# Low parts one chunk sooner in a layer and an output projection, and the short convolution's first root behind the last decays

## The chip, the cores and the metric

The kernel runs on one core of one Trainium2 chip. The metric is the device time of one execution in microseconds. Three runs before the change took 1665.22, 1665.50 and 1666.05 us (median 1665.5).

## The reference

The input is a sequence of 256 tokens (width 1024) with 256 context tokens. A first block has two layers of attention, each followed by a feed-forward part with a three-tap convolution in its gate. A second block has one layer (a chunked state-space scan beside a short-convolution branch), then a mixture of 16 experts. The parts that the change touches:

```python
def conv_ffn(h, w_gate, w_up, conv_w, conv_b, w_down):
    g = h @ w_gate
    gp = jnp.pad(g, ((0, 0), (1, 1), (0, 0)))
    g = gp[:, :-2] * conv_w[0] + gp[:, 1:-1] * conv_w[1] + gp[:, 2:] * conv_w[2] + conv_b
    return (jax.nn.silu(g) * (h @ w_up)) @ w_down

def short_conv_branch(gate_b, gate_c, h, conv_w, norm_g):
    v = causal_dwconv(gate_c * h, conv_w)
    return group_rmsnorm(gate_b * v, norm_g, SC_GROUPS)      # 16 groups of 64 columns

    proj = u @ w_in[l]
    y_ssd = ssd_branch(...)
    y_sc = short_conv_branch(proj[..., o_dt:o_b], proj[..., o_b:o_c], proj[..., o_c:], sc_conv_w[l], sc_norm[l])
    h = h + jnp.concatenate([y_ssd, y_sc], axis=-1) @ w_out[l]
```

`group_rmsnorm` divides each group of columns by the root of its mean square; all is in fp32.

## The kernel before

Everything lies with features on the 128 partitions and tokens along the free axis: 512 or 256 tokens in the first block, 272 (16 extra tokens in front) in the second. A weight matrix comes in chunks of 1 MB (128 x 2048) or 704 KB (128 x 1408) into a ring of three slots. A product in fp32 is made of three cheaper ones: the weight is split into a high part `WH` (a rounded copy, made by ScalarE in `act_high`, L514) and a low part `WL` (weight minus high part, made by VectorE, DVE for short, in `dve_low`, L524), and the activations into `HH` and `HL`. TensorE adds high x high (L539), high x low (L540) and low x high (L541).

There is no scheduler. Each engine's program is written out by hand in the order in which it runs, with semaphore waits on named marks. `act_high(e, n)` makes the high parts up to chunk n + 2; it waits until the chunk has landed and until TensorE has used the chunk three before it. `dve_low(e, n)` makes the low parts up to chunk n + 1; a third argument moves this end. A wait for a high part inside `dve_low` holds up all that DVE has behind it.

**The feed-forward part of the second layer** (256 tokens, `pe_ffn`, `act_ffn`, `dve_ffn` with l = 1, 915 to 1120 us in the trace). There are 22 gate/up chunks f in two halves of 11; each gives one tile of 128 hidden features, 48 matmuls. A stage f is, on ScalarE: the high part of chunk f + 2, the convolution's middle tap (L980), silu (L985), the high part of the product (L989), and in stages 0 to 7 a residual put off until there (L784). On DVE: a low part, the two outer taps (L1009, L1012), the product with the up half (L1016, once TensorE is through with chunk f), the low part of the product (L1019). After 11 chunks come eight down chunks; the first of them needs all 11 hidden tiles, one after the other, and waits for each tile's L1019.

**The end of the scan** (1225 to 1345 us). `pe_second_half` computes 24 tiles of the input projection, three for each of eight short-convolution tiles x, and runs `pe_scan(f - 1)` after tile f; `act_scan` and `dve_scan` are the same steps on the other engines. From step 5 on, a step starts the decays of one of 16 heads and finishes the output of an earlier one; the last decays, of head 15, are in step 20. When the squares of the tiles x = 0 to 5 are summed (L2151, one 16 x 272 row block), ScalarE takes the root (L2170) and DVE the reciprocal (L2176), both at the head of step 20. TensorE spreads the result (L2192) in steps 21 and 22, ahead of what else these steps hold; DVE and ScalarE normalise with it and split it (L2210, L2200, L2205). The root needs another activation table than the decays' exponential. Tiles 6 and 7 have a form by quarters: the 272 tokens are cut in four pieces of 68, each on 32 partitions of its own (L2160, L2187).

**The output projection** (`pe_wout`, `dve_wout`, `dve_last_tiles`). Its second half (k from the short convolution) comes first, in four chunks. Two of them are begun without tiles 6 and 7, whose sums, root (L2167), reciprocal (L2176) and spread (L2187) come in between; the state-space branch's group norm (L2458, L2464, L2520, L2555) is spread behind them.

Of the kernel before, what the change touches and what calls it, by code (L numbers as in the profile page):

```python
# [10 lines left out]
ACT = mybir.ActivationFunctionType  # L11
# [6 lines left out]
NT = 272  # L18
# [303 lines left out]
class Marks:  # L322
# [10 lines left out]
    def up(self, name, *key):  # L333
        signal = name.split(".")[0]
        assert self.home.setdefault(signal, self.engine) == self.engine, name
        n = self.count[signal] = self.count.get(signal, 0) + 1
        assert self.value.setdefault((name,) + key, n) == n, (name, key)
        return (self.final[signal] if self.final else None), 1

    def at(self, name, *key):  # L340
        if not self.final:
            return None, 1
        return self.final[name.split(".")[0]], self.value[(name,) + key]
# [38 lines left out]
def build(nc, wts, xin, meta, vecs, conds, csts, out):  # L382
# [3 lines left out]
    index = {key: n for n, (key, _) in enumerate(plan)}  # L386

    with ExitStack() as ctx:
# [48 lines left out]
        def C(name, n=None):  # L437
            return cst[:, cat[name][0]:cat[name][0] + (n or cat[name][1])]

        def B(*key):  # L440
            return ps[:, banks.of[key], :]
# [74 lines left out]
        def dve_low(e, n, ahead=2):  # L516
            short = plan[n][0][0] == "gu" and n + 1 < len(plan) and plan[n + 1][0][0] == "mod"
            for i in range(low_at[0], min(n + (3 if short else ahead), len(plan))):
                low_at[0] = i + 1
                if whole[i]:  # L520
                    continue
                hi, lo = split_parts(i)
                e.wait_ge(*at("high", i))
                e.tensor_tensor(lo, raw(i), hi.bitcast(F32), ALU.subtract).then_inc(*up("low", i))  # L524
# [440 lines left out]
        def through(l, f):  # L965
            return index["gu", l, f + 2] + 1 - index["gu", l, f]
# [29 lines left out]
        def dve_ffn(e, F_, gt_from, fold_next=None):  # L996
            l, n = F_.l, F_.n
            H2 = ffn_parts(n)
            nh = n // 256
            for half in range(2):  # L1000
                for i in range(HALF):
                    f = HALF * half + i
                    z = f % 3
                    c = index["gu", l, f]
                    g3 = B("gate", l, f)[:, 0:n].rearrange("p (s t) -> p s t", s=nh)
                    t3 = F_.T[:, z, :].rearrange("p (s t) -> p s t", s=nh)
                    dve_low(e, c, through(l, f) if f < 2 else 2)
                    e.wait_ge(*at("middle", l, f))
                    e.scalar_tensor_tensor(out=t3[:, :, 1:256], in0=g3[:, :, 0:255], scalar=V(f"cw{l}", f),  # L1009
                                           in1=t3[:, :, 1:256], op0=ALU.mult, op1=ALU.add).then_inc(*up("conv", l, f, 0))  # L1010
                    e.wait_ge(*at("conv", l, f, 0))
                    e.scalar_tensor_tensor(out=t3[:, :, 0:255], in0=g3[:, :, 1:256], scalar=V(f"cw{l}", 44 + f),  # L1012
                                           in1=t3[:, :, 0:255], op0=ALU.mult, op1=ALU.add).then_inc(*up("conv", l, f, 1))
                    e.wait_ge(*at("silu", l, f))
                    e.wait_ge(*at("used", c))
                    e.tensor_tensor(F_.SG[:, z, :], F_.SG[:, z, :], B("up", l, f)[:, 0:n],  # L1016
                                    ALU.mult).then_inc(*up("gated", l, f))
                    e.wait_ge(*at("part_high", l, f))
                    e.tensor_tensor(H2[1][:, i, :], F_.SG[:, z, :], H2[0][:, i, :].bitcast(F32),  # L1019
                                    ALU.subtract).then_inc(*up("part_low", l, f))  # L1020
                    if l == 0 and f in MOD_AT:
                        dve_mod(e, 1, MOD_AT[f])
                if l == 0:
                    dve_mod_end(e)
                if half and fold_next:
                    dve_fold(e, *fold_next)
                key = ("down", l, half)
                dve_out(e, key, n, 1, l, 40, F_.tag if half else key,
                        ("y", ("down", l, 0)) if half else ("residual", gt_from))
# [1114 lines left out]
        def pe_sc_sum(e, x, first, last):  # L2144
            b = bank(e, "sc_sum", first) if x == first else banks.of["sc_sum", first]
            r = 2 * (x - first)
            e.wait_ge(*at("sc_square", x))
            if first:
                t = pe_quarters(e, b, C("strip")[:, 14 - r:46 - r], CG[:, x % 2, :], x == first, x == last)
            else:  # L2150
                t = e.matmul(ps[0:16, b, 0:NT], C("strip")[:, 14 - r:30 - r], CG[:, x % 2, :], start=x == first,  # L2151
                             stop=x == last)
            t.then_inc(*up("sc_sum", x))
            if x == last:
                banks.give(b, "root.sc", first)

        def pe_quarters(e, b, strip, x, start, stop):
            q = NT // 4
            for g in range(4):
                t = e.matmul(ps[32 * g:32 * g + 32, b, 0:q], strip, x[:, q * g:q * g + q], start=start, stop=stop)  # L2160
            return t

        def act_sc_root(e, first, last):
            e.wait_ge(*at("sc_sum", last))
            if first:
                e.wait_ge(*at("spread.sc", 5))
                e.activation(sc_quarter, B("sc_sum", first)[:, 0:NT // 4], ACT.Sqrt, bias=EPS6,  # L2167
                             scale=1.0).then_inc(*up("root.sc", first))
                return
            e.activation(sc_root[0:16, :], B("sc_sum", first)[0:16, 0:NT], ACT.Sqrt, bias=EPS6[0:16, :],  # L2170
                         scale=1.0).then_inc(*up("root.sc", first))

        def dve_sc_inverse(e, first):
            row = sc_quarter if first else sc_root[0:16, :]
            e.wait_ge(*at("root.sc", first))
            e.reciprocal(row, row).then_inc(*up("inverse.sc", first))  # L2176

        def pe_sc_norm(e, first, last, of):
            e.wait_ge(*at("inverse.sc", of))
            for x in range(first, last + 1):  # L2180
                b = bank(e, "spread.sc", x)
                if of:
                    q = NT // 4
                    for g in range(4):
                        for h in range(2):
                            c = 32 * g + 2 * (x - of) + h
                            t = e.matmul(ps[64 * h:64 * h + 64, b, q * g:q * g + q], ident[:, c:c + 1].to_broadcast([128, 64]),  # L2187
                                         sc_quarter, start=True, stop=True)
                else:
                    for h in range(2):  # L2190
                        c = 2 * x + h
                        t = e.matmul(ps[64 * h:64 * h + 64, b, 0:NT], ident[0:16, c:c + 1].to_broadcast([16, 64]),  # L2192
                                     sc_root[0:16, :], start=True, stop=True)
                t.then_inc(*up("spread.sc", x))
                banks.give(b, "sc_unit", x)

# [192 lines left out]
                pe_sc_sum(e, x, 0 if x < 6 else 6, 5 if x < 6 else 7)  # L2389

        def act_scan(e, f):
            if f == 20:
                act_sc_root(e, 0, 5)
            act_sc_tile(e, f)
            if f in (21, 22):
                act_sc_norm(e, 3 * f - 63, 3 * f - 61)
            if f >= 5:
                step_heads(f - 5, lambda h: act_head_decay(e, h), lambda h: act_head_out(e, h))

        def dve_scan(e, f):  # L2400
            if f == 20:
                dve_sc_inverse(e, 0)
            dve_sc_tile(e, f)
            if f in (21, 22):
                dve_sc_norm(e, 3 * f - 63, 3 * f - 61)
            if f == 0:
                dve_decay_sums(e)
            elif f < 5:
                dve_group_cb(e, f - 1)
                if f < 4:  # L2410
                    dve_token_x(e, f - 1)
            else:
                step_heads(f - 5, lambda h: dve_head_decay(e, h), lambda h: dve_head_out(e, h))
# [48 lines left out]
        def dve_last_tiles(e):  # L2462
            e.wait_ge(*at("root.group"))
            e.reciprocal(sd_root, sd_root).then_inc(*up("inverse.group"))  # L2464
            dve_sc_inverse(e, 6)
            dve_sc_norm(e, 6, 7)

        def pe_wout_tiles(e, half, i, order):
# [960 lines left out]
```

## Time and profile before

| | |
|---|---|
| median of three runs | 1665.5 us |
| the profiled execution | 1665.6 us |
| its span, first to last instruction | 1663.8 us |
| TensorE busy (matmul) | 1590.2 us, 96% |
| VectorE busy | 830.3 us, 50% |
| ScalarE busy | 735.2 us, 44% |
| mean granted TensorE clock | 0.989 |
| L524 (low parts), 134 instructions | 281.6 us busy; waits for L514 before them 146.7 us |
| L539 waiting for L524, whole span | 11.0 us |

A busy share is a mean over stages with different limits. A busy TensorE is one that has matmuls in flight, so what a change is worth is read from its idle stretches, and from who ended them. The rows further down have, in a timeline, the start, the duration, engine, line, operation, output and inputs, and in brackets the idle time before with its releaser.

### The profile page before, as it was taken

What the parts mean: (1) busy time and instruction counts of PE and PEld (TensorE: products, weight loads), DVE (VectorE), ACT (ScalarE), POOL (GpSimd) and SP (SyncE); (2) the same over time, 40 slices, a digit from 0 to 9 for tenths busy, and PEclk for the clock granted to TensorE, in tenths of its full rate; (3) what the DMA queues carried; (4) which work ended last, traced back from release to release, by engine and by line L of the source; (5) the groups of instructions that cost most, each with busy time, mean ns of one, the idle gap of its engine ahead of it and who ended that gap; (6) DMA issues with size and microseconds to landing.
All of it is one profiled execution on the core that took longest, in us unless ns stands there. A gap on an engine that the chain in (4) does not pass through costs nothing.

```text
span 1663.8 us, 26843 instructions
## 1 busy us (share of the span) xinstructions
PE 1590.2 (96%) x11188; PEld 1227.4 (74%) x11188; DVE 830.3 (50%) x1461; ACT 735.2 (44%) x1140; POOL 0.9 (0%) x5
## 2 busy tenths in 40 slices
PE   8999989999999999999889899999999989999987
PEld 5646567777787778689768899998988778535443
DVE  2536664634333344542675766655677764312223
ACT  3444552633213332442463654546545543455443
POOL 0000000000000000000000000000000000000000
PEclk9999999999999999999999999999999999999999
DMA  9412523254334433423202345452442227799995
GB/s 390 150 39 102 203 102 104 99 198 157 135 106 164 190 121 99 173 77 127 101 1 77 129 159 208 166 177 99 167 140 102 77 102 289 318 403 421 421 420 209
DMA packets 43133, 287.89 MB, mean 173 GB/s; under 512 B 4849, under 2 KB 6001, under 8 KB 12161
## 3 DMA queue, kind: packets, MB, share of 16 engines
q1 hardware_dynamic: 42832, 285.99, 45.6%
q8 instruction: 92, 1.51, 0.4%
q14 instruction: 33, 0.26, 0.0%
q10 hardware_dynamic: 144, 0.06, 0.0%
q0 software_dynamic: 32, 0.07, 0.0%
HBM read 285.05 MB, written 1.05 MB: 172 GB/s over the span
## 4 chain that ended last, share of the span: by engine, by line
PE 80%; DVE 9%; ACT 5%; DMA 4%; issue 2%; DVEq 0%; SPq 0%; ACTq 0%
PE ps L539 17%; PE ps L540 16%; PE ps L541 16%; PE ps L2936 7%; DMA deep<-wts 4%; DVE WL L524 2%; PE ps L584 2%; PE ps L2796 1%; PE ps L1553 1%; PE ps L1524 1%; PE ps L1455 1%; PE ps L564 1%; PE ps L702 1%; PE ps L1632 1%; PE ps L1631 1%
## 5 line engine op out<-in xcount | busy, mean ns | idle before, releaser
L539 PE MATMUL ps<-HH,WH 128*128 128x512 f32 (+2 forms) x1488 | 495.5, 333 | 20.8 <-DVE WL L524 11.0
L541 PE MATMUL ps<-HH,WL 128*128 128x512 f32 (+2 forms) x1488 | 483.8, 325 | 0.0
L540 PE MATMUL ps<-HL,WH 128*128 128x512 f32 (+2 forms) x1488 | 483.6, 325 | 0.0
L524 DVE TENSOR_TENSOR WL<-ring,WH 128x2048 fp32r<-128x2048 f32 (+2 forms) x134 | 281.6, 2104 | 146.7 <-ACT WH L514 146.7
L539 PEld LDWEIGHTS ps<-HH,WH 128*128 128x128 f32 x1488 | 284.4, 191 | 70.6 <-issue 31.6
L541 PEld LDWEIGHTS ps<-HH,WL 128*128 128x128 f32 x1488 | 284.3, 191 | 21.8
L514 ACT ACTIVATE WH<-ring 128x2048 fp32r<-128x2048 f32 (+2 forms) x134 | 235.8, 1761 | 144.5 <-DMA ring<-wts 77.1
L540 PEld LDWEIGHTS ps<-HL,WH 128*128 128x128 f32 x1488 | 284.9, 191 | 19.7
L2936 PE MATMUL ps<-deep,arena 128*32 128x512 f32 (+1 forms) x872 | 114.0, 593 | 10.7 <-ACT late_x L2922 5.6
L539 PE MATMUL ps<-parts,WH 128*128 128x512 f32 (+1 forms) x352 | 119.7, 340 | 0.0
L540 PE MATMUL ps<-parts,WH 128*128 128x512 f32 (+1 forms) x352 | 118.4, 336 | 0.0
L541 PE MATMUL ps<-parts,WL 128*128 128x512 f32 (+1 forms) x352 | 118.2, 336 | 0.0
L2936 PEld LDWEIGHTS ps<-deep,arena 128*32 128x32 f32 x872 | 41.6, 110 | 78.6 <-issue 78.5
L918 DVE SCALAR_TENSOR_TENSOR X<-ps,modv,X 128x256 f32<-128x256 f32 x72 | 32.4, 480 | 124.5 <-PE ps L541 124.5
L539 PEld LDWEIGHTS ps<-parts,WH 128*128 128x128 f32 x352 | 66.7, 190 | 9.0 <-issue 1.8
L541 PEld LDWEIGHTS ps<-parts,WL 128*128 128x128 f32 x352 | 66.8, 190 | 6.9
L540 PEld LDWEIGHTS ps<-parts,WH 128*128 128x128 f32 x352 | 66.8, 190 | 6.7
L2922 ACT ACTIVATE deep<-deep 128x2048 f32 x23 | 43.9, 1911 | 47.1 <-DMA deep<-wts 32.1
L985 ACT ACTIVATE arena<-arena 128x512 f32<-128x512 f32 (+1 forms) x44 | 23.1, 525 | 84.9 <-DVE arena L1012 84.9
L2936 PE MATMUL ps<-late_x,arena 128*32 128x512 f32 x128 | 57.7, 593 | 0.0
L2936 PE MATMUL ps<-deep,tail 128*32 128x512 f32 (+1 forms) x448 | 57.2, 594 | 0.3 <-ACT late_x L2922 0.2
L1499 ACT ACTIVATE arena<-ps,small 128x512 f32<-128x512 f32 (+1 forms) x64 | 36.4, 578 | 44.8 <-DVE small L1480 22.8
(400 smaller groups left out, 2107.3 us busy)
## 6 DMA issues: line engine op xcount, KB each, us to landing
ring<-wts SPq DMA_DIRECT2D x138, 1024.0 KB, 4.9
deep<-wts SPq DMA_DIRECT2D x92, 1024.0 KB, 16.5
ring<-wts SPq DMA_DIRECT2D x32, 704.0 KB, 4.0
arena<-wts SPq DMA_DIRECT2D x8, 1024.0 KB, 15.4
ring<-wts SPq DMA_DIRECT2D x4, 672.0 KB, 13.7
X<-xin SPq DMA_DIRECT2D x4, 512.0 KB, 16.4
ahead<-wts SPq DMA_DIRECT2D x2, 1024.0 KB, 8.7
deep<-wts SPq DMA_DIRECT2D x4, 512.0 KB, 20.6
```

What stands on the lines that cost most here:

```text
L514: e.activation(split_parts(i)[0], raw(i), ACT.Copy).then_inc(*up("high", i))
L524: e.tensor_tensor(lo, raw(i), hi.bitcast(F32), ALU.subtract).then_inc(*up("low", i))
L539: e.matmul(o, w[0][:, cols], x[0], start=k == 0, stop=False)
L540: e.matmul(o, w[0][:, cols], x[1], start=False, stop=False)
L541: return e.matmul(o, w[1][:, cols], x[0], start=False, stop=k == nk - 1)
L564: e.matmul(o[1][m], v[0][:, 256 * k + 128 * m:256 * k + 128 * m + 128], at_k(x, k)[h], start=k == h == 0, stop=False)
L584: t = e.matmul(ps[32 * j:32 * j + 32, b, :], scond[:, 2 * k:2 * k + 32], w[:, 512 * j:512 * j + 512], start=k == 0, stop=k == 7)
L918: t = e.scalar_tensor_tensor(out=X[:, j, a:z], in0=B("out", key, j)[:, a:z], scalar=modv[l][:, gt + j, s:s + 1], in1=X[:, j, a:z], op0=ALU ...
L985: e.activation(F_.SG[:, z, :], F_.T[:, z, :], ACT.Silu).then_inc(*up("silu", l, f))
L1499: t = e.activation(PA3[z][s][:, n * q:n * q + n], B("scores", j, s)[:, n * q:n * q + n], ACT.Exp, bias=column(nm, j, s, q), scale=sc, accu ...
L2922: e.activation(OTHER[q % 2], m[:, bass.ds(v + a, SLOT)], ACT.Copy).then_inc(*up("other", q))
L2936: r = e.matmul(o[c, :], x[:, c], w, start=start, stop=stop)
```

## The change

There are four edits.
1. In the second layer's feed-forward part, `dve_low` runs one chunk further from f = 2 on: to chunk f + 2, whose high part ScalarE makes in the same stage.
2. The sums of squares, the root, the reciprocal and the spread of the first six short-convolution tiles take the form by quarters that the last two tiles have.
3. Root and reciprocal of these six move from the head of step 20 to step 21, behind the short-convolution tile and the decays of step 20. With it they come behind the high and low part that each engine makes between steps 20 and 21. TensorE's order stays.
4. In `dve_last_tiles` the low part of the third output chunk is made between the last reciprocal and the last two normalisations.

```diff
                     c = index["gu", l, f]
                     g3 = B("gate", l, f)[:, 0:n].rearrange("p (s t) -> p s t", s=nh)
                     t3 = F_.T[:, z, :].rearrange("p (s t) -> p s t", s=nh)
-                    dve_low(e, c, through(l, f) if f < 2 else 2)
-                    dve_low(e, c, through(l, f) if f < 2 else 2)
+                    dve_low(e, c, through(l, f) if f < 2 else 2 + l)
...
-            if first:
-                t = pe_quarters(e, b, C("strip")[:, 14 - r:46 - r], CG[:, x % 2, :], x == first, x == last)
-            else:
-                t = e.matmul(ps[0:16, b, 0:NT], C("strip")[:, 14 - r:30 - r], CG[:, x % 2, :], start=x == first,
-                             stop=x == last)
+            t = pe_quarters(e, b, C("strip")[:, 14 - r:46 - r], CG[:, x % 2, :], x == first, x == last)
...
-            e.activation(sc_root[0:16, :], B("sc_sum", first)[0:16, 0:NT], ACT.Sqrt, bias=EPS6[0:16, :],
+            e.activation(sc_quarter, B("sc_sum", first)[:, 0:NT // 4], ACT.Sqrt, bias=EPS6,
                          scale=1.0).then_inc(*up("root.sc", first))
...
-            e.reciprocal(row, row).then_inc(*up("inverse.sc", first))
+            e.reciprocal(sc_quarter, sc_quarter).then_inc(*up("inverse.sc", first))
...
-                    for h in range(2):
-                        c = 2 * x + h
-                        t = e.matmul(ps[64 * h:64 * h + 64, b, 0:NT], ident[0:16, c:c + 1].to_broadcast([16, 64]),
-                                     sc_root[0:16, :], start=True, stop=True)
+                for g in range(4):
+                    for h in range(2):
+                        c = 32 * g + 2 * (x - of) + h
+                        t = e.matmul(ps[64 * h:64 * h + 64, b, q * g:q * g + q], ident[:, c:c + 1].to_broadcast([128, 64]),
+                                     sc_quarter, start=True, stop=True)
...
         def act_scan(e, f):
-            if f == 20:
+            act_sc_tile(e, f)
+            if f == 21:
                 act_sc_root(e, 0, 5)
-            act_sc_tile(e, f)
...
         def dve_scan(e, f):
-            if f == 20:
+            dve_sc_tile(e, f)
+            if f == 21:
                 dve_sc_inverse(e, 0)
-            dve_sc_tile(e, f)
...
             dve_sc_inverse(e, 6)
+            dve_low(e, index["wout", 1, 1])
             dve_sc_norm(e, 6, 7)
```

DVE's order in stages 1 to 3 of the second layer's feed-forward part, before (L524 is a low part; what an instruction waits for is in brackets):

```order
L524 TENSOR_TENSOR WL<-ring,WH 128x2048 [waits high]
L1009 SCALAR_TENSOR_TENSOR arena<-ps,vec,arena 128x255 [waits middle]
L1012 SCALAR_TENSOR_TENSOR arena<-ps,vec,arena 128x255 [waits conv]
L1016 TENSOR_TENSOR arena<-arena,ps 128x256 [waits used,silu]
L1019 TENSOR_TENSOR parts<-arena,parts 128x256 [waits part_high]
L1009 SCALAR_TENSOR_TENSOR arena<-ps,vec,arena 128x255 [waits middle]
L1012 SCALAR_TENSOR_TENSOR arena<-ps,vec,arena 128x255 [waits conv]
L1016 TENSOR_TENSOR arena<-arena,ps 128x256 [waits used,silu]
L1019 TENSOR_TENSOR parts<-arena,parts 128x256 [waits part_high]
L524 TENSOR_TENSOR WL<-ring,WH 128x2048 [waits high]
L1009 SCALAR_TENSOR_TENSOR arena<-ps,vec,arena 128x255 [waits middle]
```

and with the change:

```order
L524 TENSOR_TENSOR WL<-ring,WH 128x2048 [waits high]
L1009 SCALAR_TENSOR_TENSOR arena<-ps,vec,arena 128x255 [waits middle]
L1012 SCALAR_TENSOR_TENSOR arena<-ps,vec,arena 128x255 [waits conv]
L1016 TENSOR_TENSOR arena<-arena,ps 128x256 [waits used,silu]
L1019 TENSOR_TENSOR parts<-arena,parts 128x256 [waits part_high]
L524 TENSOR_TENSOR WL<-ring,WH 128x2048 [waits high]
L1009 SCALAR_TENSOR_TENSOR arena<-ps,vec,arena 128x255 [waits middle]
L1012 SCALAR_TENSOR_TENSOR arena<-ps,vec,arena 128x255 [waits conv]
L1016 TENSOR_TENSOR arena<-arena,ps 128x256 [waits used,silu]
L1019 TENSOR_TENSOR parts<-arena,parts 128x256 [waits part_high]
L524 TENSOR_TENSOR WL<-ring,WH 128x2048 [waits high]
L1009 SCALAR_TENSOR_TENSOR arena<-ps,vec,arena 128x255 [waits middle]
```

A low part now stands at the head of stage 2 as well, and each later stage's low part is that of the chunk after.

DVE's order from step 20 on, before (L2176 is the reciprocal, L2129 to L2141 short-convolution tile 6, L2313 to L2320 the decays of head 15, which wait for ScalarE's exponentials):

```order
L2176 RECIPROCAL X<-X 16x272 [waits root]
L2129 TENSOR_TENSOR X<-X,ps 128x272 [waits tile,sc_gate]
L2133 TENSOR_SCALAR X<-X,vec 128x272 [waits sc_out]
L2135 SCALAR_TENSOR_TENSOR X<-X,vec 128x271 [waits sc_out]
L2138 SCALAR_TENSOR_TENSOR X<-X,vec 128x270 [waits sc_out]
L2141 TENSOR_TENSOR arena<-X,ps 128x272 [waits sc_out]
L2313 TENSOR_SCALAR X<-ps,arena 16x16 [waits head_exp,head_out,head,decay_bias]
L2314 TENSOR_SCALAR cst<-ps,arena 128x128
L2315 TENSOR_SCALAR cst<-ps,arena 128x128
L2319 TENSOR_TENSOR cst<-cst,arena 16x272 [waits cb_masked,head_exp]
L2320 TENSOR_TENSOR cst<-cst,arena 128x384
```

and with the change, from the end of the decays of head 15 (L2305, L2306) to the first normalisations (L2196; L2168 is the reciprocal):

```order
L2305 TENSOR_TENSOR cst<-cst,arena 16x272 [waits cb_masked,head_exp]
L2306 TENSOR_TENSOR cst<-cst,arena 128x384
L2337 SCALAR_TENSOR_TENSOR arena<-arena,vec,ps 128x272 [waits head_out]
L2340 TENSOR_TENSOR arena<-arena 128x272 [waits y_gated]
L524 TENSOR_TENSOR WL<-ring,WH 128x2048 [waits high]
L2168 RECIPROCAL X<-X 128x68 [waits root]
L2196 SCALAR_TENSOR_TENSOR arena<-arena,vec,ps 128x272 [waits spread] x2
```

The reciprocal has gone from before tile 6 to behind the decays, the output of head 13 (L2337, L2340) and a low part.

ScalarE's order there, before (L2170 is the root, L2119 the square of tile 6, L2296 to L2302 the exponentials of head 15):

```order
L2170 ACT_TABLE_LOAD
L2170 ACTIVATE X<-ps,cst 16x272 [waits sc_sum]
L2119 ACTIVATE X<-arena 128x272 [waits sc_out]
L2296 ACT_TABLE_LOAD [waits head_out]
L2296 ACTIVATE cst<-X 16x16 [waits head_mixed]
L2297 ACTIVATE cst<-ps,arena 16x128
L2298 ACTIVATE cst<-ps,arena 16x128
L2299 ACTIVATE cst<-ps,arena 128x128
L2301 ACTIVATE cst<-cst 128x128
L2302 ACTIVATE cst<-cst 128x128
L2360 ACTIVATE arena<-arena 128x272 [waits y_gated]
L514 ACTIVATE WH<-ring 128x2048 [waits used,s_w0]
```

and with the change (L2163 is the root):

```order
L2119 ACTIVATE X<-arena 128x272 [waits sc_out]
L2282 ACTIVATE cst<-X 16x16 [waits head_out,head_mixed]
L2283 ACTIVATE cst<-ps,arena 16x128
L2284 ACTIVATE cst<-ps,arena 16x128
L2285 ACTIVATE cst<-ps,arena 128x128
L2287 ACTIVATE cst<-cst 128x128
L2288 ACTIVATE cst<-cst 128x128
L2346 ACTIVATE arena<-arena 128x272 [waits y_gated]
L514 ACTIVATE WH<-ring 128x2048 [waits used,s_w0]
L2163 ACT_TABLE_LOAD
L2163 ACTIVATE X<-ps,cst 128x68 [waits sc_sum]
```

The root is behind the exponentials and behind a high part (L514), and one table load stands where two stood. The load ahead of L2458 is gone as well, since the root's table stays.

## Rows read from the trace of the kernel before

**Rows 1.** The page, part 4: the chain that ended last, by engine.
```profile
PE 80%; DVE 9%; ACT 5%; DMA 4%; issue 2%; DVEq 0%; SPq 0%; ACTq 0%
```

**Rows 2.** TensorE's waits, 925 to 1085 us: total, times, longest.
```profile
PE ps L539 <- DVE WL L524: 4.5, 2, 4.0
```

**Rows 3.** Timeline of ACT, 929 to 976 us: start, duration, instruction.
```profile
929.48 1.90 ACT L514 ACTIVATE WH<-ring 128x2048 fp32r<-128x2048 f32 x1
...
935.87 0.58 ACT L784 ACTIVATE X<-arena,lnc 128x256 f32<-128x256 f32 x1
936.36 1.90 ACT L514 ACTIVATE WH<-ring 128x2048 fp32r<-128x2048 f32 x1
...
941.49 1.89 ACT L514 ACTIVATE WH<-ring 128x2048 fp32r<-128x2048 f32 x1
...
975.95 1.37 ACT L514 ACTIVATE WH<-ring 128x1408 fp32r<-128x1408 f32 x1
```

**Rows 4.** Timeline of DVE, 931 to 1030 us; in brackets, idle time before.
```profile
931.40 2.29 DVE L524 TENSOR_TENSOR WL<-ring,WH 128x2048 fp32r<-128x2048 f32 x1 [1.87 <-ACT WH L514]
...
935.09 0.42 DVE L1016 TENSOR_TENSOR arena<-arena,ps 128x256 f32<-128x256 f32 x1 [0.48 <-ACT arena L985]
...
982.18 1.62 DVE L524 TENSOR_TENSOR WL<-ring,WH 128x1408 fp32r<-128x1408 f32 x1
...
1024.13 0.42 DVE L1016 TENSOR_TENSOR arena<-arena,ps 128x256 f32<-128x256 f32 x1 [1.35 <-PE ps L541]
...
1029.89 0.42 DVE L1016 TENSOR_TENSOR arena<-arena,ps 128x256 f32<-128x256 f32 x1 [1.32 <-PE ps L541]
```

**Rows 5.** Timeline of TensorE: chunk 4, and the first down chunk.
```profile
943.81 0.58 PE L539 MATMUL ps<-HH,WH 128*128 128x256 f32 x1 [4.05 <-DVE WL L524]
...
986.42 0.28 PE L539 MATMUL ps<-parts,WH 128*128 128x256 f32 x1
```

**Rows 6.** Windows: length, busy time of PE, PEld, DVE, ACT, POOL, clock, DMA.
```profile
943.80:948.80 5.00, 4.99 (x23) 5.00 (x24) 3.93 (x5) 3.16 (x5) 0.00 (x0) 0.50 0.62 210
1358.50:1361.70 3.20, 3.11 (x13) 3.12 (x14) 2.21 (x7) 1.12 (x3) 0.00 (x0) 0.50 0.70 220
861.00:875.00 14.00, 10.34 (x64) 9.02 (x64) 5.29 (x15) 8.65 (x20) 0.00 (x0) 1.00 0.00 1
```

**Rows 7.** All waits of DVE, 1240 to 1321 us.
```profile
DVE arena L2319 <- ACT arena L2302: 18.2, 12, 2.5
...
```

**Rows 8.** Timeline of DVE at the end of the scan.
```profile
1318.52 0.43 DVE L2319 TENSOR_TENSOR arena<-arena 16x272 f32<-16x272 f32 x1 [1.43 <-ACT arena L2302]
...
1320.31 1.84 DVE L2176 RECIPROCAL X<-X 16x272 f32<-16x272 f32 x1 [0.89 <-ACT X L2170]
...
1327.55 0.43 DVE L2319 TENSOR_TENSOR cst<-cst,arena 16x272 f32<-16x272 f32 x1 [2.52 <-ACT cst L2302]
...
1334.15 0.90 DVE L2210 SCALAR_TENSOR_TENSOR arena<-arena,vec,ps 128x272 f32<-128x272 f32 x2
...
1344.03 0.58 DVE L2464 RECIPROCAL arena<-arena 128x68 f32<-128x68 f32 x1 [1.73 <-ACT arena L2458]
...
1347.81 0.97 DVE L2210 SCALAR_TENSOR_TENSOR arena<-arena,vec,ps 128x272 f32<-128x272 f32 x2 [2.76 <-PE ps L2187]
```

**Rows 9.** Timeline of ACT, the same place.
```profile
1329.70 1.90 ACT L514 ACTIVATE WH<-ring 128x2048 fp32r<-128x2048 f32 x1
...
1342.38 1.28 ACT L2458 ACT_TABLE_LOAD   x1
```

**Rows 10.** Timeline of TensorE, the same place.
```profile
1312.26 0.63 PE L2151 MATMUL ps<-X,cst 128*16 128x272 f32 x2
...
1322.21 1.13 PE L2192 MATMUL ps<-X,cst 16*64 16x272 f32 x8 [0.26 <-DVE X L2176]
...
1347.06 1.17 PE L2187 MATMUL ps<-X,cst 128*64 128x68 f32 x32
...
1358.59 0.60 PE L539 MATMUL ps<-HH,WH 128*128 128x272 f32 x1 [4.18 <-DVE WL L524]
```

More of the change, by code:

```diff
@@ L2166, in act_sc_root @@
                 e.wait_ge(*at("spread.sc", 5))
-                e.activation(sc_quarter, B("sc_sum", first)[:, 0:NT // 4], ACT.Sqrt, bias=EPS6,
-                             scale=1.0).then_inc(*up("root.sc", first))
-                return
-            e.activation(sc_root[0:16, :], B("sc_sum", first)[0:16, 0:NT], ACT.Sqrt, bias=EPS6[0:16, :],
+            e.activation(sc_quarter, B("sc_sum", first)[:, 0:NT // 4], ACT.Sqrt, bias=EPS6,
                          scale=1.0).then_inc(*up("root.sc", first))
         def dve_sc_inverse(e, first):
-            row = sc_quarter if first else sc_root[0:16, :]
             e.wait_ge(*at("root.sc", first))
-            e.reciprocal(row, row).then_inc(*up("inverse.sc", first))
+            e.reciprocal(sc_quarter, sc_quarter).then_inc(*up("inverse.sc", first))
         def pe_sc_norm(e, first, last, of):
             e.wait_ge(*at("inverse.sc", of))
+            q = NT // 4
             for x in range(first, last + 1):
                 b = bank(e, "spread.sc", x)
-                if of:
-                    q = NT // 4
-                    for g in range(4):
-                        for h in range(2):
[L2186 to L2189, printed above, removed]
+                for g in range(4):
                     for h in range(2):
-                        c = 2 * x + h
-                        t = e.matmul(ps[64 * h:64 * h + 64, b, 0:NT], ident[0:16, c:c + 1].to_broadcast([16, 64]),
-                                     sc_root[0:16, :], start=True, stop=True)
+                        c = 32 * g + 2 * (x - of) + h
+                        t = e.matmul(ps[64 * h:64 * h + 64, b, q * g:q * g + q], ident[:, c:c + 1].to_broadcast([128, 64]),
+                                     sc_quarter, start=True, stop=True)
                 t.then_inc(*up("spread.sc", x))
```

## The prediction

> **What bounds the kernel now.** I read the page's chain of waits first. TensorE carries 80% of it, VectorE (DVE) 9%, ScalarE (ACT) 5% [rows 1]. So a change counts where TensorE stands still or where its clock falls. Next came the table of TensorE's waits for the second layer's feed-forward part (925 to 1085 us). It has two waits in 160 us, 4.5 us in all, both for a low part that DVE makes in L524 [rows 2]. Then I read the timelines of ACT, DVE and TensorE around the long wait [rows 3 to 5], and the same three around the end of the scan, 1312 to 1359 us [rows 8 to 10]. The second place has a stall at 1322, a row of small ones, and 4.18 us at 1358.59.
>
> The chip's part in it: after the waits of 4.05 and 4.18 us the granted clock was at the 1.2 GHz level (0.50) for 5.0 and 3.2 us; with TensorE busy for 10.3 of 14 us in shorter gaps it stayed at 2.4 GHz (1.00) [rows 6]. A stretch at half rate loses half its length, so 2.5 and 1.6 us.
>
> **Part 1, the layer's gate/up chunks (2 becomes 3).** The long wait is chunk 4's: ACT makes its high part at 936.36, DVE its low part only a stage later, and TensorE starts at 943.81 [rows 3, 5]. With the change DVE makes it in stage 2, straight behind its high part. Stage 1 has just this order today: high part at 929.48, low part at 931.40, 1.92 later [rows 3, 4]. So chunk 4's low part starts at 936.36 + 1.92 = 938.28, and at 938.28 + 2.28 + 0.06 = 940.62 TensorE can start. It gains 3.2 us and the 2.5 us of half rate.
>
> What it costs is the order of a stage. Today DVE's low part for f+1 rests on a high part made one stage ago, so ACT's high part and DVE's low part run side by side. A stage (high part to high part) is 941.49 - 936.36 = 5.13 us, less than TensorE's chunk of 1029.89 - 1024.13 = 5.76 us, and TensorE bounds [rows 3, 4]. With the change the low part for f+2 waits for the high part of its own stage, and the two convolution steps, silu, product, high and low part of f stand behind it on DVE. That is stage 1's order, and stage 1 took 936.36 - 929.48 = 6.88 us [rows 3]: 1.92 to the low part, 2.20 for it, 1.49 for the convolutions and silu up to the product at 935.09 [rows 4], and 1.27 for product, high part and residual. After stage 7 the residual (L784, 0.49 us from its start to the next instruction's) is gone: 6.39. So DVE and ACT together need more than TensorE's 5.76 in every stage.
>
> First half: TensorE starts chunk 4 at 940.62 and is there ready for each next one 1.12 us too soon. Chunk 10 starts at 940.62 + 6 x 6.88 = 981.90 and ends at 987.66; now the down projection starts at 986.42 [rows 5], 1.2 earlier. Then the down projection needs the low part of hidden tile 10. The product of stage 8 is at 983.21 (981.90 less 2.34 for chunk 10's low part, then 2.20 and 1.49). Stages 9 and 10 have the short chunks, whose high part takes 1.37 and low part 1.62, 0.53 and 0.66 less [rows 3, 4], so 5.20 each: product at 993.61, its low part done 1.36 later, 994.97. TensorE is there after ten of eleven steps of three matmuls, 0.12 each (48 make its 5.76), at 987.66 + 3.60 = 991.26: a new wait of 3.7 us. Together 4.9 us.
>
> Second half: here DVE is level with TensorE at the start (its product waits for TensorE in every stage now [rows 4]), and a low part two chunks ahead has 6 us of cover. It falls behind by 0.5 in the first stage, by 6.39 - 5.76 = 0.63 in eight more and wins 0.56 back in each of the last two: 4.4 us. TensorE doesn't wait for the weights, but again for the last hidden tile: 0.25 (handing over) + 4.4 + 1.36 - 3.60 = 2.4 us. Part 1: 4.9 + 2.4 = +7.3 us. The 3.7 us wait lies near those that dropped the clock, so half rate costs between 0 and 2.5; I take the nearer-lying 1.6: +8.9. The gaps of 1.12 in 6.88 us leave TensorE busy for 84%, more than in the 14 us that stayed at 1.00 [rows 6], so nothing for them.
>
> A rule of the Trainium skill speaks against this part. ACT and DVE take a queue strictly in order, only TensorE pulls a weight load ahead (TensorE: Matmul & The Clock Gate, "Architectural detail"). The trace agrees: in stage 1 the convolution came behind the low part, though its input was there. If DVE could pass the waiting low part, the stage would stay at 5.13 and part 1 would be -5.7.
>
> **Part 2, root and inverse of the first six short-convolution tiles.** Sums by quarters: a full-width sum's two passes take 0.63 us [rows 10]; six of them can save at most 3.8 us, all before the stall at 1322, where TensorE would only wait longer: 0. What moves is on DVE and ACT; from 1240 to 1321 DVE waits for ACT alone, most of it in 12 waits of this kind [rows 7], so it isn't TensorE that sets when the root comes. Without the wait of 0.89 and the reciprocal of 1.84, DVE comes to the next tile 2.73 sooner; without the table load between, it waits 1.43 for the exponentials and not 2.52 [rows 8]: 3.82 in all. So ACT's L514 starts at 1329.70 - 3.82 = 1325.88 [rows 9]. But now the root is behind it: 1.90, then load to reciprocal 1.65 (1342.38 to 1344.03), then 0.58 [rows 8, 9]: 1330.03. TensorE's spread stands where it stood, before the scan's last tile, and starts at 1330.1, not at 1322.21 [rows 10]. It is nearly 8 us later, after a stall long enough for half rate.
> Then three spreads (two take 1.17, so 1.75), the tile (24 matmuls, 0.127 each by the timeline) and 1.6 for half rate: 1336.5. The next spread reaches DVE 0.75 later, at 1337.25, where its second three normalisations start at 1334.15 now [rows 8, 10]: **3.1 us late** for all that follows. Half rate from 0 to 2.5 makes that 1.5 to 4.0.
>
> The skill puts a switch of the activation table at 1283 ns and a drain of about 1380 ns, 2.66 us (ScalarE: Activation LUTs, "What ACT_TABLE_LOAD costs"). The row has 1.28 us [rows 9], and the 1.65 up to the reciprocal hold the square root too, so there is no drain in them. By the page the root would be 1.4 later and the result +1.4.
>
> **Part 3, third output chunk.** DVE waits 2.76 us for the spread at 1347.81 [rows 8]. The low part (2.28) fits in there, for the spread moves with TensorE. Without that cover it would hold up the normalisation by up to 2.3. It removes the 4.18 us wait and its 1.6 of half rate [rows 6, 10]. Next late is the fourth chunk's low part, still in its old place behind two pairs of normalisations; by counting on through the timeline it is about 0.5 late (0 to 1.5). Parts 2 and 3: 3.1 - 4.18 - 1.6 + 0.5 = -2.2, with the bounds -3.8 to +0.5.
>
> **Sum.** 8.9 - 2.2 = +6.7 us. The profiled execution took 1665.6 us (span 1663.8), the median is 1665.5: 1672.2. The experts behind it stream their weights into space that this work frees, so the shift goes through.
>
> **Rivals.** A change under 0.2% (3.3 us) can't be told from none here.
> - B, the giving back is smaller: the wait at the second half's end is hidden, or the clock holds. 7.3 - 2.4 - 2.2 = +2.7 to +5: about 1669. For it: that wait rests on a lag added up over eleven stages. Against: each stage has its rows.
> - C, the clock falls in the regular gaps or a second time: two more stretches at half rate, +5: 1677. Against: [rows 6], third row.
> - D, faster: the early low parts take away the 4.05 us wait with its half rate, and nothing is given back, because ACT's high part is there when DVE asks. -5.7 - 2.2: 1657.6. It decides from a stage shorter than 5.76 us. Against: 6.88 in stage 1.
> - E, the scan's end gains more than I think: the stall at 1322 doesn't lengthen, since the root gets in sooner. Then -3.8 instead of +3.1 there, and the sum is about 0: 1665.3. Against: the root is now behind a high part of 1.90 us, and the spread has kept its place in TensorE's order.
>
> **Numbers.** A 0.64, B 0.13, C 0.09, D 0.06, E 0.08. Forecast 1672.2, its own range 1669 to 1675; with B, most of C and near E 1667 to 1677. Slower by over 0.2% (above 1668.8): A nearly all, C, over half of B: 0.80. Within: 0.13. Faster: 0.07.
>
> **What would show it.** In the feed-forward part: DVE waiting for ACT before nearly every L524, TensorE starting chunk 4 at about 940.6, six waits of 1.1, then one of 3.7 in the first down chunk and 2.4 in the second half's. In the scan: TensorE idle for 8 to 12 us ahead of the first spread, one table load in place of three, the 4.18 us wait gone. I am wrong if the L524 stages are no longer than 5.8 us, or if the spread isn't held up.

## The result, and the profile after

| | before | after |
|---|---|---|
| median, five runs each | 1665.55 us | 1673.56 us |
| span of the profiled execution | 1663.8 us | 1670.8 us |
| L524 waiting for L514 (DVE) | 146.7 us | 173.5 us |
| TensorE busy | 1590.2 us | 1587.0 us |

The ratio is 1.0047 (95% interval 1.0036 to 1.0058), so the change costs 8.0 us, from 6.0 to 9.7. The forecast was 1672.2. The two profiled executions differ by 7.0 us, for the one after entered the feed-forward part 1.98 us sooner, from code that is the same in both. Below, "at the same instruction" means the start after minus the start before, each counted from the start of its own execution. One execution of run 9 took 2610.38 us at a mean granted clock of 0.556, against 0.99 in the other seven, and its time is left out.

The chain of waits shows the shift from TensorE to the two helpers [rows 1]. The page's part 4 after:

```profile
PE 77%; DVE 10%; ACT 7%; DMA 4%; issue 2%; SPq 0%; DVEq 0%; ACTq 0%
```

TensorE's waits between 925 and 1100 us (after; total, times, longest), against one long and one short in [rows 2]:

```profile
PE ps L539 <- DVE WL L524: 6.6, 8, 0.9
PE ps L539 <- DVE parts L1019: 5.8, 2, 3.5
```

The 4.0 has gone. In its place stand eight waits of at most 0.9 for low parts, and two, 3.5 and 2.3, for the last hidden tile of either half (the forecast had six of 1.1, then 3.7 and 2.4).

TensorE, timeline after: chunk 4, chunk 10, the down projection, its wait in the first half and in the second [rows 5]:

```profile
938.67 0.39 PE L539 MATMUL ps<-HH,WH 128*128 128x256 f32 x1 [0.88 <-DVE WL L524]
...
979.99 0.39 PE L539 MATMUL ps<-HH,WH 128*128 128x256 f32 x1 [0.87 <-DVE WL L524]
...
985.84 0.28 PE L539 MATMUL ps<-parts,WH 128*128 128x256 f32 x1
...
993.11 0.38 PE L539 MATMUL ps<-parts,WH 128*128 128x256 f32 x1 [3.51 <-DVE parts L1019]
...
1092.22 0.39 PE L539 MATMUL ps<-parts,WH 128*128 128x256 f32 x1 [2.33 <-DVE parts L1019]
```

Chunk 4 starts at 938.67, with the 1.98 added back 940.65 (forecast 940.62; before 943.81). Chunks 4 to 10 then follow 6.89 us apart.

DVE's timeline after says why [rows 4]: each low part waits 1.87 for the high part of its own stage, and the product comes after it.

```profile
929.43 2.29 DVE L524 TENSOR_TENSOR WL<-ring,WH 128x2048 fp32r<-128x2048 f32 x1 [1.87 <-ACT WH L514]
...
936.32 2.29 DVE L524 TENSOR_TENSOR WL<-ring,WH 128x2048 fp32r<-128x2048 f32 x1 [1.87 <-ACT WH L514]
...
943.21 2.29 DVE L524 TENSOR_TENSOR WL<-ring,WH 128x2048 fp32r<-128x2048 f32 x1 [1.87 <-ACT WH L514]
...
992.63 0.43 DVE L1019 TENSOR_TENSOR parts<-arena,parts 128x256 fp32r<-128x256 f32 x1 [0.48 <-ACT parts L989]
```

All of DVE's waits from 930 to 984 us, after (total, times, longest):

```profile
DVE WL L524 <- ACT WH L514: 15.8, 9, 1.9
DVE arena L1016 <- ACT arena L985: 3.9, 8, 0.5
DVE parts L1019 <- ACT parts L989: 3.9, 8, 0.5
```

There is no wait for TensorE in this list. In the same stretch before, DVE waited for TensorE six times:

```profile
DVE arena L1016 <- PE ps L541: 7.1, 6, 1.3
DVE parts L1019 <- ACT parts L989: 4.3, 9, 0.5
```

In that stretch ACT's waits after are for DVE alone too, so neither of the two helpers waits for TensorE any longer.

TensorE's clock behind the two long waits, windows after (length, busy time of PE, clock, DMA share, GB/s):

```profile
993.00:994.00 1.00, 0.89 (x7) 1.00 0.77 315
994.00:995.00 1.00, 1.00 (x8) 0.69 0.00 0
995.00:996.00 1.00, 1.00 (x7) 0.50 0.00 0
996.00:997.00 1.00, 1.00 (x7) 0.50 0.57 56
997.00:998.00 1.00, 1.00 (x7) 0.60 0.52 180
...
1093.00:1094.00 1.00, 1.00 (x8) 0.69 0.02 6
1094.00:1095.00 1.00, 1.00 (x7) 0.50 0.00 0
1095.00:1096.00 1.00, 1.00 (x7) 0.50 0.33 28
1096.00:1097.00 1.00, 1.00 (x7) 0.61 0.62 180
```

The clock stood at 0.50 behind both waits, the one of 2.33 us too. It fell more than a microsecond after TensorE had begun again (at 993.11 and at 1092.22).

What each stretch cost is read from TensorE's own start times. The second half's first down matmul, before and after (the same instruction, ahead of the second wait):

```profile
1081.46 0.28 PE L539 MATMUL ps<-parts,WH 128*128 128x256 f32 x1
...
1086.12 0.28 PE L539 MATMUL ps<-parts,WH 128*128 128x256 f32 x1
```

TensorE is 4.66 late there. The two matmuls that end the long waits start at 990.02 and 1085.06 before, so they are 3.09 and 7.16 late, and behind the part the shift is 8.76. So half rate cost 4.66 - 3.09 = 1.57 behind the first wait and 8.76 - 7.16 = 1.60 behind the second.

At the scan's end, after: ACT, DVE and TensorE (timelines; [rows 8 to 10]):

```profile
1334.75 1.89 ACT L514 ACTIVATE WH<-ring 128x2048 fp32r<-128x2048 f32 x1
1336.66 1.28 ACT L2163 ACT_TABLE_LOAD   x1
1337.96 0.32 ACT L2163 ACTIVATE X<-ps,cst 128x68 f32<-128x68 f32 x1
```

```profile
1338.31 0.58 DVE L2168 RECIPROCAL X<-X 128x68 f32<-128x68 f32 x1 [1.72 <-ACT X L2163]
...
1346.12 0.97 DVE L2196 SCALAR_TENSOR_TENSOR arena<-arena,vec,ps 128x272 f32<-128x272 f32 x2 [2.71 <-PE ps L2178]
...
1354.58 0.58 DVE L2450 RECIPROCAL arena<-arena 128x68 f32<-128x68 f32 x1 [0.30 <-ACT arena L2444]
```

```profile
1338.94 2.99 PE L2178 MATMUL ps<-X,cst 128*64 128x68 f32 x48 [8.34 <-DVE X L2168]
...
1341.86 0.59 PE L539 MATMUL ps<-HH,WH 128*128 128x272 f32 x1
```

The execution after enters the scan 8.80 late. With that taken off, the spread starts at 1330.14 (forecast 1330.1) and the second three normalisations at 1337.32 (forecast 1337.25, before 1334.15). Of TensorE's 4.18 us wait in the output projection 0.7 is left:

```profile
PE ps L539 <- DVE HL L2191: 1.1, 1, 1.1
PE ps L539 <- DVE WL L524: 0.7, 1, 0.7
```

At the same instructions the shift runs: -1.98 ahead of the feed-forward part, +4.66 on TensorE after its first half, +8.76 behind it, +11.97 at the scan's last tile, +7.07 behind the output projection, and so to the end. So part 1 cost 10.74, part 2 3.2, and part 3 gave 4.9.

### The profile page after: what moved, and what is told of

It reads as the page before. It is cut to its first block, busy times and chain, and to the rows that moved or that the text cites. A ratio compares the mean times of both kernels' runs of the same rounds, so it can differ in the third digit from the quotient of the medians.

```text
span 1670.8 us, 27057 instructions
## 1 busy us (share of the span) xinstructions
PE 1587.0 (95%) x11296; PEld 1229.8 (74%) x11296; DVE 830.4 (50%) x1461; ACT 731.1 (44%) x1138; POOL 0.9 (0%) x5
## 4 chain that ended last, share of the span: by engine, by line
PE 77%; DVE 10%; ACT 7%; DMA 4%; issue 2%; SPq 0%; DVEq 0%; ACTq 0%
PE ps L539 16%; PE ps L540 15%; PE ps L541 15%; PE ps L2923 7%; DMA deep<-wts 4%; DVE WL L524 3%; PE ps L584 2%; ACT WH L514 2%; PE ps L2783 1%; PE ps L1553 1%; PE ps L1524 1%; PE ps L1455 1%; PE ps L564 1%; PE ps L702 1%; PE ps L1632 1%
## 5 line engine op out<-in xcount | busy, mean ns | idle before, releaser
L524 DVE TENSOR_TENSOR WL<-ring,WH 128x2048 fp32r<-128x2048 f32 (+2 forms) x134 | 281.7, 2105 | 173.5 <-ACT WH L514 173.5
L514 ACT ACTIVATE WH<-ring 128x2048 fp32r<-128x2048 f32 (+2 forms) x134 | 235.7, 1761 | 143.4 <-PE ps L541 75.1
```

Of the source, the lines that this page charges most:

```text
L514: e.activation(split_parts(i)[0], raw(i), ACT.Copy).then_inc(*up("high", i))
```

## The experiments

All were timed beside the kernel before on the same chip; the differences are of those medians, and the ratios have their 95% intervals in brackets. Runs 1 to 4 stood beside a median of 1666.68, runs 5 to 8 of 1666.0, runs 9 and 10 of 1665.7.

**Run 1, the change without part 1.** The edit, in the changed kernel:

```diff
-                    dve_low(e, c, through(l, f) if f < 2 else 2 + l)
+                    dve_low(e, c, through(l, f) if f < 2 else 2)
```

> The change without its first part: the layer's gate/up chunks keep 2, root and sums moved and the third output chunk's low part early. The two traces differ by 7.0 us; read apart at common instructions, the feed-forward part added 10.7 us (from -1.98 to +8.76), the scan 3.2 and the output projection gave back 4.9. Theory (the parts add up): 1665.5 - 1.7 = 1663.8, from 1662.5 to 1665. Rival (the parts meet: the scan's end loses because it starts late against the weights): more than 3 us faster, below 1662.5. Rival (the scan's shift eats what the low part brings): 1665.5 or above.

Measured: 1664.06, 2.6 us faster than before; ratio 0.9983 (0.9973 to 0.9992). Parts 2 and 3 gain, by about what the forecast gave them (2.2). At the same instructions its trace has them at 1.1: part 2 costs 3.75 (from +3.58 to +7.33) and part 3 gives 4.9 (to +2.44).

**Run 2, part 1 alone,** one line replaced in the kernel before:

```diff
-                    dve_low(e, c, through(l, f) if f < 2 else 2)
+                    dve_low(e, c, through(l, f) if f < 2 else 2 + l)
```

> The kernel before with the first part alone (2 becomes 2 + l for the gate/up chunks). Theory: a stage of 6.88 us against TensorE's 5.76 gives +4.9 in the first half and +2.4 in the second, and the half rate behind the two long waits (not one, as I had it) 2.2 and 1.2: +10.7, so 1676, from 1674.5 to 1677.5. Rival (part of the 10.7 is a chance of that one execution): +8.9 or less, below 1674.5.

Measured: 1677.35, 10.7 us slower; ratio 1.0059 (1.0045 to 1.0074). Its waits in the feed-forward part are the same as after the full change, 6.6 in eight and 5.8 in two. In its trace the shift on TensorE is 10.4, from +0.48 to +10.88. The 2.2 and 1.2 of half rate in the expectation are a wrong split: TensorE's own starts give 1.57 and 1.60 after the change, and 1.4 and 1.4 in run 2. Run 1 and run 2 add up to the change: 10.7 - 2.6 = 8.1 against the 8.0 measured. The parts don't meet.

**Run 3, part 3 alone:**

```diff
             dve_sc_inverse(e, 6)
+            dve_low(e, index["wout", 1, 1])
             dve_sc_norm(e, 6, 7)
```

> The kernel before with the third part alone: the low part of the third output chunk ahead of the last two normalisations. Theory: the 4.18 us wait and its 1.6 at half rate go, 0.5 to 1 is late elsewhere: -4.8 to -5.3, so 1660.5, from 1659.7 to 1661.5. Rival (the cover for the low part is there only because the spread is late with the root moved): about -3, 1662.5. If the difference to the run with parts two and three is 3 to 3.5 us, the moved root costs what was forecast (3.1).

Measured: 1661.65, 5.0 us faster; ratio 0.9972 (0.9962 to 0.9981). The low part lies in the wait of 2.76 that was there before, of which 0.64 is left. DVE's timeline of run 3:

```profile
1344.58 2.23 DVE L524 TENSOR_TENSOR WL<-ring,WH 128x2048 fp32r<-128x2048 f32 x1
1347.45 0.97 DVE L2210 SCALAR_TENSOR_TENSOR arena<-arena,vec,ps 128x272 f32<-128x272 f32 x2 [0.64 <-PE ps L2187]
```

So by the medians part 2 costs 5.0 - 2.6 = 2.4, where 3.1 was forecast and the two traces that have it show 3.2 (after) and 3.75 (run 1). The medians' intervals are too wide to choose between these.

**Run 4, the quarters alone:** part 2 without its move. In the changed kernel, with parts 1 and 3 undone:

```diff
+            if f == 20:
+                dve_sc_inverse(e, 0)
             dve_sc_tile(e, f)
-            if f == 21:
-                dve_sc_inverse(e, 0)
```

and the same for `act_sc_root`.

> The kernel before with sums, root and inverse by quarters, but root and inverse in their old place, ahead of tile 6, and the low part in its old place. Theory: only the width counts there. The reciprocal is 0.58 instead of 1.84 us on an engine that is bound through ACT and not by TensorE: -1.3 for all that follows, so 1664.2, from 1663.6 to 1665. Rival (TensorE sets the scan's pace, DVE's time is covered): 1665.5. Rival (the narrow sums save TensorE six times 0.3 to 0.6 us as well): 1662.5.

Measured: 1664.53, 2.15 us faster; ratio 0.9987 (0.9978 to 0.9996). In its trace the scan's last tiles shift from +0.20 to -1.22, 1.4 in all, where the reciprocal stands, and not before it: the six narrower sums alone brought nothing. The median's further 0.7 lies within its interval (0.6 to 3.7 us). DVE's timeline of run 4, against 1.84 in [rows 8]:

```profile
1320.35 0.58 DVE L2168 RECIPROCAL X<-X 128x68 f32<-128x68 f32 x1 [0.73 <-ACT X L2163]
```

The form by quarters is a gain, and the new place loses it and more: with the form it costs 2.4 by the medians, where the form alone gives 2.15.

**Run 5, ACT's high parts ahead as well.** Run 2 and

```diff
-                    act_high(e, c, through(l, f) if f < 2 else 3)
+                    act_high(e, c, through(l, f) if f < 2 else 3 + l)
```

> The first part alone, and in the second layer ACT's high parts too one chunk further ahead from stage 2 on (3 becomes 3 + l). Theory (the 6.88 us stage comes from DVE's low part waiting for a high part of its own stage): the low part finds its high part made a stage ago, a stage is back at about 5.1 us, and what is left is the gain at chunk 4, 3.2 and 2.5 of half rate: -5.7 against the kernel before, -5 to -6; stage 2 alone, with two high parts, takes about 7.6. Against the first part alone that is 16 us. Rival (DVE's own work is too much for a stage): like the first part alone, +10. Rival (the high part now waits for the weights or for its place, used until TensorE has done the chunk): between 0 and +5.

Measured: 1664.64, 1.4 us faster; ratio 0.9992 (0.9983 to 1.0001), which can't be told from none; against run 2 12 us faster. The first theory holds for the stage: DVE's low parts wait no longer, 5.13 apart in run 5:

```profile
943.30 2.28 DVE L524 TENSOR_TENSOR WL<-ring,WH 128x2048 fp32r<-128x2048 f32 x1
...
948.43 2.28 DVE L524 TENSOR_TENSOR WL<-ring,WH 128x2048 fp32r<-128x2048 f32 x1
```

Its size fails, since the third rival is true as well. The high part now waits until TensorE has used chunk f, while the middle tap (L980) needs only the gate half of it, the first half of the chunk's matmuls, and stands behind. ACT in run 5:

```profile
1026.01 1.92 ACT L514 ACTIVATE WH<-ring 128x2048 fp32r<-128x2048 f32 x1 [1.00 <-PE ps L541]
1027.83 0.54 ACT L980 ACTIVATE arena<-ps,vec 128x256 f32<-128x256 f32 x1
```

TensorE waited twice, 2.5 us in all, for the last hidden tiles; the clock stayed at 1.00 behind both. At the same instructions the feed-forward part brings 2.4 (from +0.02 to -2.38). Of this 1.1 is lost again in the output projection, whose code is the same: behind its long wait TensorE worked 5.7 us at half rate, where it was 3.2 before [rows 6].

**Run 6, the turn of part 1:** the first layer gets 3, the second keeps 2.

```diff
-                    dve_low(e, c, through(l, f) if f < 2 else 2)
+                    dve_low(e, c, through(l, f) if f < 2 else 3 - l)
```

> The first part turned round: the first layer's gate/up chunks get 3, the second layer keeps 2. A chunk of 512 columns keeps TensorE busy for about 12 us (products 12.1 us apart in the first layer), and the same chain of high part, low part, convolution, product takes about 7 to 9. Theory (the stage must be longer than TensorE's chunk to cost): within 1 us of the kernel before. Rival (a low part two chunks ahead costs by itself, by the ring's places or the weights' transfer): +3 or more.

Measured: 1666.43, 0.4 us slower; ratio 1.0002 (0.9993 to 1.0011). The same edit is free where TensorE's chunk takes 12 us (512 tokens, not 256). TensorE waits for nothing in the first layer's feed-forward part (320 to 640 us), before and in this run. DVE's waits for high parts hardly move: 44.0 us in nine between 320 and 435 us, against 44.1.

**Run 7, the spread one step later.** Run 1 and, on all three engines:

```diff
-            if f in (21, 22):
-                pe_sc_norm(e, 3 * f - 63, 3 * f - 61, 0)
+            if f in (22, 23):
+                pe_sc_norm(e, 3 * f - 66, 3 * f - 64, 0)
```

> Parts two and three with the spreads and their normalisations one step later (22 and 23 in place of 21 and 22), so that the scan's last tile stands ahead of the first spread in TensorE's order. Theory (the spread in its old place holds TensorE up): the 8.3 us wait gets shorter by the tile's 3.05, and DVE's second three normalisations come 3 to 4 sooner: 3 to 4 faster than the run with parts two and three, 6 faster than the kernel before. Rival (DVE has the tile's convolution ahead of the last normalisations now, 2.4 us): no faster than with parts two and three.

Measured: 1664.64, 1.4 us faster than before; ratio 0.9992 (0.9983 to 1.0001), so no better than run 1, where 3 to 4 us were expected. The theory fell. With the spread out of its way TensorE waited 7.72 us all the same, now in the scan's last tile:

```profile
1329.18 0.60 PE L539 MATMUL ps<-HH,WH 128*128 128x272 f32 x1 [7.72 <-ACT X L2163]
```

L2163 is the root. The kernel keeps the sums' bank of PSUM (TensorE's output memory) until the root has read them, and the next tile is written to that bank. So the root's place held up TensorE twice over, by the spread and by the bank. The forecast had only the first, which came first and gave the right number.

**Run 8, three in stage 2 alone:**

```diff
-                    dve_low(e, c, through(l, f) if f < 2 else 2)
+                    dve_low(e, c, through(l, f) if f < 2 else 3 if l and f == 2 else 2)
```

> The kernel before, with 3 in stage 2 of the second layer alone and 2 in all others. Theory (the low part two ahead buys one stage and loses its lead at once): stage 3 makes no low part, chunk 5's comes in stage 4, which starts at 936.36 + 6.88 + 5.13 = 948.4, done at 950.6; TensorE wants it at 946.4. The wait of 4 us moves from chunk 4 to chunk 5, and the end is 1.1 late (0.5 to 1.8) against the kernel before. Rival (what the first part gives at chunk 4 stays if the later stages are short again): -5.7.

Measured: 1667.42, 1.4 us slower; ratio 1.0008 (0.9999 to 1.0017), at the edge of what can be told. The trace is plainer: at the same instruction +0.00 ahead of the feed-forward part and +1.16 behind it. TensorE in run 8, chunks 4 and 5:

```profile
940.64 0.39 PE L539 MATMUL ps<-HH,WH 128*128 128x256 f32 x1 [0.88 <-DVE WL L524]
...
950.71 0.58 PE L539 MATMUL ps<-HH,WH 128*128 128x256 f32 x1 [4.05 <-DVE WL L524]
```

The wait of 4.05 moved one chunk on.

**Run 9, the middle tap first.** Run 5, but from stage 3 on ACT makes the high part behind L980:

```diff
-                    act_high(e, c, through(l, f) if f < 2 else 3 + l)
+                    if not (l and f > 2):
+                        act_high(e, c, through(l, f) if f < 2 else 3 + l)
                     ...
+                    if l and f > 2:
+                        act_high(e, c, 4)
                     e.wait_ge(*at("conv", l, f, 1))
```

> Like the run with high and low parts ahead, but from stage 3 on ACT takes the convolution's first step (L980) ahead of the high part. There, in the second half, the high part waited for its place until TensorE had done chunk f (at 1026.0) and the step, whose gate half was long there, stood behind it: the product came 4.8 after TensorE's end instead of 0.05, so TensorE waited 1.2 for the last hidden tile of either half. Theory: now the convolution is done beside TensorE's second half, only silu stands behind the high part, the last low part is there 3.05 after the chunk's end, inside the 3.60 that TensorE has work for, and both waits of 1.2 go: 4.5 to 6 faster than the kernel before, 2 to 3.5 faster than the run it mends. Rival (the waits come from the late start of the halves, not from the order on ACT): no faster than that run.

Measured: 1660.86, 4.8 us faster; ratio 0.9972 (0.9961 to 0.9982). All of TensorE's waits in the feed-forward part (925 to 1110 us) of run 9:

```profile
PE ps L539 <- DVE WL L524: 1.4, 2, 0.9
```

The two of 1.2 are gone. At the same instructions the part brings 5.4 (from +0.24 to -5.13), against 2.4 in run 5.

**Run 10, all that helped:** run 9, run 4 and run 3 together.

> All that the runs pointed to: the feed-forward part as in the run beside this, sums, root and inverse by quarters in their old place, and the low part of the third output chunk early. Theory (the pieces stand far apart and add): -5.2, -1.3 and -5.0, together 11.5 faster than the kernel before, 10 to 13, and 18 to 20 faster than the changed kernel. Rival (with the scan earlier the low part's cover of 2.76 shrinks, or the experts' weights take some of it back): 8 to 10.

Measured: 1653.89, 11.8 us faster than the kernel before; ratio 0.9930 (0.9917 to 0.9942), and some 20 us faster than the changed kernel. The gains of the three alone come to 4.8 + 2.15 + 5.0 = 12.0. TensorE's waits between 1200 and 1375 us in run 10:

```profile
PE ps L539 <- DVE WL L524: 2.7, 3, 1.4
PE ps L539 <- ACT cst L2288: 2.0, 1, 2.0
PE ps L539 <- DVE HL L2194: 1.1, 1, 1.1
```

## Why the prediction was right, step by step

- **The 6.88 us stage** is what the trace shows (6.89), chunk 4's start too (0.03 off). Run 5 shows the cause: with the high part made a stage earlier, the stage is 5.13 again. Run 6 fits the condition that the order costs only where TensorE's chunk is shorter than the chain: with a chunk of 12 us it cost nothing. Run 8 shows that the lead is spent again in one stage.
- **The waits for the last hidden tile** came at the forecast place and size: 3.51 (3.7) and 2.33 (2.4). By TensorE's starts they cost 3.67 (3.09 + 0.58) and 2.50 (7.16 - 4.66), since the idle time in brackets counts from the end of the matmul before. The first half lost 1.40 up to the down projection (1.2 forecast).
- **Half rate behind the second wait is the mis-sized term.** I took 1.6 for the first wait and nothing for the second. The first half cost 6.64 on TensorE: 1.40 for the order, 3.67 for the wait and 1.57 at half rate, against 6.5 forecast. The second cost 4.10: 2.50 for the wait, as forecast, and 1.60 at half rate, where the sum had nothing. That is nearly all of what part 1 cost beyond the forecast (10.7 against 8.9). It is the second stretch that rival C named, though not at five microseconds. That the first came out at 1.6 is partly luck: the same kind of stretch varies by about a microsecond, as the last section shows.
- **The clock in shorter gaps.** The forecast took its safety from the third row of [rows 6], and the gaps of 0.9 us did leave the clock at 1.00. But the row itself doesn't hold in every execution: in run 4 the clock fell in that stretch (last section).
- **Strict order.** The forecast read it from stage 1, and that reading fails: the middle tap, which the convolution waits for, ended on ACT at 931.83, and DVE had begun the low part at 931.40 already. So the low part was ready first, and an engine free to choose would have begun with it too. What a run shows is ACT's side: in run 5 ACT stood idle for 1.00 us with the middle tap behind the waiting high part, and in run 9, which takes the tap first, TensorE's two waits of 1.2 are gone.
- **Part 2** is right at each of its points: the spread at 1330.14, TensorE idle for 8.34, and DVE 3.2 late (3.75 in run 1). Run 4 bears out that the narrow sums bring nothing and that the reciprocal's 1.26 shows. Run 7 shows a second thing that held TensorE there, which I had not seen.
- **The table load** took 1.28 again, and from its start to the reciprocal 1.65, the square root in it. With the Trainium skill's further drain of about 1380 ns (ScalarE: Activation LUTs, "What ACT_TABLE_LOAD costs") an estimate for the reciprocal is 1338.31 + 1.38, about 1339.7. It started at 1338.31, so the trace does not agree.
- **Part 3**: its two sides give 4.9 at the same instructions, forecast 4.18 + 1.6 - 0.5 = 5.3. Run 3 gives 5.0, and its cover was there without part 2.
- **The rivals.** B fell with the 2.33 us wait, D with the stage, E with the idle 8.34.

By the terms the sum is 10.7 + 3.2 - 4.9 = 9.0, the median says 8.0 and the profile 7.0, which has the 1.98 from ahead of the change in it. The forecast of 6.7 came within its range because the terms were right but for one, and that one was 1.6 short; of the other 0.7 part 3 has 0.4 (4.9 for 5.3). That the median lies only 1.3 above the forecast, and not 2.3 as by the terms, is luck: the interval of 6.0 to 9.7 has room for both.

## What to carry to other kernels

When two engines in strict order hand work to each other, an early request is only free if the giver made the thing a stage ago. Moving one side by a stage moves the other into the chain, and the chain must then be shorter than the bound engine's step. Move both sides, and then look at what each moved step now waits for and what stands behind it (run 5 against run 9). A result that comes later holds up also what wants its buffer (run 7).

## What the runs showed of the hardware

The same code lost different amounts to half rate. After the wait of about 4 us at chunk 4, which several of the kernels share, TensorE worked at a granted clock of 0.50 for 5.0 us before the change [rows 6], and for about 3 us in run 3, where it began again at 944.28. At the same instructions this alone moved run 3 by 0.88 us. TensorE's windows in run 3:

```profile
944.00:945.00 1.00, 0.72 (x3) 0.50 0.00 0
945.00:946.00 1.00, 1.00 (x7) 0.50 0.86 147
946.00:947.00 1.00, 1.00 (x6) 0.50 0.79 311
947.00:948.00 1.00, 1.00 (x9) 0.85 1.02 434
```

The output projection's wait shows it as well, at 3.2 us before and 5.7 in run 5. So in these traces a term of half rate has a spread of about a microsecond, and one execution doesn't give it more closely. And the clock can fall after the wait is over, as behind the 3.51 and the 2.33 here; a window on the wait alone would miss it. The eight regular gaps of up to 0.9 us, 6.9 us apart, did not lower it; one window after:

```profile
950.00:960.00 10.00, 8.26 (x67) 1.00 0.31 107
```

Whether a gap lowers the clock also varies. The stretch from 861 to 875 us, with one gap of 1.88 us, kept 1.00 before [rows 6, third row]. In run 4, whose code is the same up to there, the mean was 0.88, since the clock stood at 0.50 from 867 to 869 us, and the run lost 1.6 us there (from -0.65 to +0.92 on TensorE):

```profile
861.00:875.00 14.00, 10.45 (x57) 0.88 0.00 1
```
